# The end of a two-block transformer kernel: the last four experts of the mixture taken apart from the loop, their sums left in PSUM

## The chip, the cores and the metric

The kernel runs on one core of a Trainium2 chip. The metric is device time in microseconds (us) of one execution, the median over several runs. Everything is fp32 in memory. TensorE (PE) multiplies, VectorE (DVE) and ScalarE (ACT) move and combine, GpSimd (POOL) takes roots, SyncE (SP) issues the DMAs of the weights and of the output.

## The reference, cut to what matters

Two transformer blocks follow each other; the second one ends with a mixture of 64 experts, added to the residual, and a last normalization. Only this end is touched.

```
def hier_moe(h, w_group, w_expert, w1, w3, w2):       # 512 tokens, D = 1024, 64 experts, top 2
    ...                                               # gates[token, 2], expert_id[token, 2]
    def expert_block(args):
        xb, e = args
        hid = jax.nn.silu(xb @ w1[e]) * (xb @ w3[e])  # w1, w3: 1024 x 256
        return hid @ w2[e]                            # w2: 256 x 1024
    ys = lax.map(expert_block, (xs, block_e)).reshape(n_slots, dm)
    ys = ys * slot_gate[:, None].astype(ys.dtype)
    out = jnp.zeros((n_tok + 1, dm), ys.dtype).at[slot_tok].add(ys)[:n_tok]
...
    x = x + hier_moe(h, ...)
    return rmsnorm(x, final_norm)
```

## The kernel before, in words

Each expert gets C = 32 places for tokens; one that has more tokens gets an extra block, in a loop behind a branch on `n_over` (the number of extra blocks). Four experts make a bunch (BUNCH = 4) of 128 places, so there are 16 bunches (BUNCHES = 16).

For each expert `b` the kernel does this:
- SP loads W1 and W3 (`gate_up_in`, two DMAs of 1 MB, six slots) and W2 (`down_in`, one DMA of 1 MB, five slots). The order on SP is the gate-and-up weights of expert e+1, then the down weights of expert e. A slot's DMA waits for the PE step that used the slot last.
- PE `gate_up` (L1769): 32 matmuls, four at a time on 32 columns of the array each, into bank 2 or 3. ACT takes the silu (L1104), DVE the product (L2500), PE transposes it (`hidden`, L1783), DVE copies that out (L2520), PE `down` (L1797): 8 matmuls of 32x256 into bank 6 or 7, one quarter of the columns for each 32 partitions. ACT and DVE copy two quarters each into the rows of `Y` (L1110 and L2506).

For each bunch the four experts' rows are brought back to tokens: ACT makes the gated high half of `Y` (`Yhi`, L1127), DVE the rest (`Ylo`, L2525), and PE multiplies both with the 128x512 one-hot places `S4` (`by_token`, L1822 and L1823, two fp32r matmuls for each of 8 tiles, tile = 128 tokens x 512 columns). DVE adds each tile from bank 0 or 1 to the residual `xres` in SBUF (L2539). The two banks alternate, so the matmul of tile i waits for the addition of tile i-2. This work of bunch g-1 is spread over the experts of bunch g.

The last bunch has nothing to be spread over. Its sum is taken once at the end in full fp32: PE multiplies `gated_places` with `Y` (L1961, 8 matmuls), DVE adds each tile (L2539), ACT sums the squares of each 128 tokens (L806), DVE and POOL make the reciprocal root (L2621, L2668), DVE scales (L2616, `finish`), and SP stores (L775 and L779). The branch on `n_over` stands on each engine between the last expert and these matmuls (L1927 on PE). In the profiled execution the loop behind it isn't run: the trace has no row of its lines.

Fillers (`idle_turns`, L1816) are matmuls whose result nobody reads.

The order on each engine is the order of the code; there is no scheduler. Engines wait for each other by semaphores.

## Time and profile before

| | us |
|---|---|
| median of 3 runs | 1454.14 (1452.13 to 1454.15) |
| span of the profiled execution | 1449.5 |
| PE busy | 1386.8 (96%) |
| DVE busy, ACT busy | 526.3, 522.3 |
| DMA | 293.22 MB, mean 202 GB/s |

No time of its own is listed for the profiled execution; two of the three runs took 1454.14 and 1454.15, which is 4.6 us more than its span, for what lies around the span. Matmuls are pipelined and their ends are modelled, so a busy share of PE says little by itself. Where an fp32 matmul stands in a row, the count is of two records for each instruction: the 32 matmuls of `gate_up` are x64.

### The profile page before, as it was taken

Reading aid. Unit: us, or ns where it says so; the run is one execution under the profiler, and the core shown is the slowest. Engines: PE = TensorE matmul, PEld = TensorE weight load, DVE = VectorE, ACT = ScalarE, POOL = GpSimd, SP = SyncE. Lnnn points to the kernel's source line nnn. Section 1 sums busy time; section 2 is a strip of 40 time slices with the busy share of each in tenths; the row PEclk is TensorE's granted clock in tenths of the full one; section 3 lists DMA queues with packets and bytes.
Section 4 is the critical chain, followed back from the end, with each engine's and each line's share of the span. In section 5 each row is a group of like instructions: output and inputs, shape, how many; then the busy total and the mean of one; then the engine's idle time right before and its main releaser. Section 6 shows DMA issues by size and latency. Waiting matters only on the chain. (4 is left out here: it accounts for less than half of the span.)

```text
span 1449.5 us, 26659 instructions
## 1 busy us (share of the span) xinstructions
PE 1386.8 (96%) x11116; PEld 1038.9 (72%) x11116; DVE 526.3 (36%) x1256; ACT 522.3 (36%) x1096; POOL 474.6 (33%) x457
## 2 busy tenths in 40 slices
PE   6999999999999999999989999999999999889986
PEld 5788886668788888888868786866666665555553
DVE  3102107752221200221244604264554554454435
ACT  4325438863422322322345533342223222222222
POOL 5334545553544444444355854410000000000000
PEclk9999999999999999999999999999999999999999
DMA  5133215304133124231232311669999999999994
GB/s 188 59 118 116 96 59 173 112 16 160 58 117 105 41 94 153 73 116 61 89 116 73 106 69 59 241 253 382 410 419 419 419 419 420 419 420 420 420 420 183
DMA packets 89561, 293.22 MB, mean 202 GB/s; under 512 B 9308, under 2 KB 38144, under 8 KB 64864
## 3 DMA queue, kind: packets, MB, share of 16 engines
q1 hardware_dynamic: 89040, 290.35, 51.9%
q8 instruction: 90, 1.47, 0.4%
q0 software_dynamic: 288, 1.05, 0.2%
q14 instruction: 31, 0.25, 0.0%
q10 hardware_dynamic: 112, 0.09, 0.0%
HBM read 289.27 MB, written 2.13 MB: 201 GB/s over the span
## 5 line engine op out<-in xcount | busy, mean ns | idle before, releaser
L496 POOL TENSOR_TENSOR wring_halves<-wring,wring_halves 128x512 fp32r<-128x512 f32 x274 | 356.6, 1306 | 379.9 <-ACT wring_halves L491 378.2
L491 ACT CAST wring_halves<-wring 128x512 fp32r<-128x512 f32 x274 | 168.3, 621 | 433.2 <-PE ps L1223 412.2
L1221 PE MATMUL ps<-wring_halves,big_halves 128*128 128x512 f32 x612 | 241.6, 395 | 3.7 <-POOL wring_halves L496 2.6
L1221 PE MATMUL ps<-hT_halves,wring_halves 128*128 128x512 f32 x480 | 187.4, 390 | 2.4 <-DVE big_halves L1981 2.4
L1222 PE MATMUL ps<-big_halves,wring_halves 128*128 128x512 f32 x480 | 186.8, 389 | 0.0
L1223 PE MATMUL ps<-hT_halves,wring_halves 128*128 128x512 f32 x480 | 186.7, 389 | 0.0
L2668 POOL TENSOR_TENSOR rstd<-rstd,half 128x1 f32<-128x1 f32 (+1 forms) x21 | 13.6, 647 | 507.7 <-DVE rstd L2621 478.5
L1222 PE MATMUL ps<-wring_halves,hT_halves 128*128 128x512 f32 x436 | 170.7, 391 | 0.0
L1223 PE MATMUL ps<-wring_halves,hT_halves 128*128 128x512 f32 x436 | 170.6, 391 | 0.0
L1221 PEld LDWEIGHTS ps<-wring_halves,big_halves 128*128 128x128 f32 x612 | 115.4, 189 | 31.9 <-POOL wring_halves L496 5.7
L1742 PE MATMUL ps<-xn,fixed 128*128 128x512 f32 x256 | 119.2, 608 | 1.1 <-DVE fixed L2416 1.1
L1221 PEld LDWEIGHTS ps<-hT_halves,wring_halves 128*128 128x128 f32 x480 | 90.1, 188 | 22.5 <-POOL wring_halves L496 2.9
L1223 PEld LDWEIGHTS ps<-hT_halves,wring_halves 128*128 128x128 f32 x480 | 90.1, 188 | 18.9
L1222 PEld LDWEIGHTS ps<-big_halves,wring_halves 128*128 128x128 f32 x480 | 90.1, 188 | 18.8 <-issue 0.2
L2506 DVE COPY arena<-ps 32x256 f32<-32x256 f32 x128 | 54.3, 425 | 120.6 <-PE ps L1797 116.0
L1223 PEld LDWEIGHTS ps<-wring_halves,hT_halves 128*128 128x128 f32 x436 | 82.3, 189 | 17.6
L1222 PEld LDWEIGHTS ps<-wring_halves,hT_halves 128*128 128x128 f32 x436 | 82.5, 189 | 16.5
L2539 DVE TENSOR_TENSOR xres<-xres,ps 128x512 f32<-128x512 f32 x128 | 82.5, 683 | 22.1 <-PE ps L1823 18.0
L2160 DVE TENSOR_TENSOR arena<-arena,ps 128x512 f32<-128x512 f32 x22 | 15.0, 684 | 195.4 <-ACT arena L971 195.4
L1742 PEld LDWEIGHTS ps<-xn,fixed 128*128 128x128 f32 x256 | 46.3, 191 | 54.6 <-issue 52.3
L1769 PE MATMUL ps<-big,arena 128*32 128x128 f32 x2048 | 65.9, 279 | 8.8 <-DMA big<-in_moe_w_dram 8.2
L1110 ACT COPY arena<-ps 32x256 f32<-32x256 f32 x128 | 46.3, 361 | 64.2 <-PE ps L1797 63.5
(348 smaller groups left out, 1986.3 us busy)
## 6 DMA issues: line engine op xcount, KB each, us to landing
big<-in_moe_w_dram SPq DMA_DIRECT2D x90, 1024.0 KB, 24.7
wring<-in_moe_w_dram SPq DMA_DIRECT2D x70, 1024.0 KB, 25.2
wring<-in_ffn_w_in_dram SPq DMA_DIRECT2D x22, 1024.0 KB, 7.3
hT<-in_moe_w_dram SPq DMA_DIRECT2D x20, 1024.0 KB, 24.3
wring<-in_fox_w_in_dram SPq DMA_DIRECT2D x7, 2048.0 KB, 8.7
wring<-in_gla_w_in_dram SPq DMA_DIRECT2D x6, 2048.0 KB, 7.9
mkv<-in_moe_w_dram SPq DMA_DIRECT2D x12, 1024.0 KB, 26.1
wring<-in_ffn_w_out_dram SPq DMA_DIRECT2D x4, 2048.0 KB, 7.8
```

The source lines that it names most:

```text
L491: act.copy(hi, src).then_inc(s_hi, 1)
L496: pool.tensor_tensor(lo, src, hi, ALU.subtract).then_inc(s_lo, 1)
L1110: last = act.copy(rows[:, n * YG:(n + 1) * YG], bank(6 + j % 2)[n * C:(n + 1) * C, 0:YG])
L1221: pe.matmul(out, lhs[1], rhs[0], start=start, stop=False)
L1222: pe.matmul(out, lhs[0], rhs[1], start=False, stop=False)
L1223: return pe.matmul(out, lhs[0], rhs[0], start=False, stop=stop)
L1742: last = pe.matmul(bank(n), one_hots(g)[1][:, t, :], xn[:, t, n * 512:(n + 1) * 512], start=(t == 0), stop=(t == T - 1))
L1769: last = pe.matmul(o[i * C:(i + 1) * C, 0:2 * HG], xeT[:, k, r * C:(r + 1) * C], w[:, :, i // 2, :, i % 2], start=(k == 0), stop=(k == KD ...
L2160: dve.tensor_tensor(prod[f % 2], sg[f % 2], bank((2 * f + 1) % 8), ALU.mult).then_inc(s_hid, 1)
L2506: last = dve.tensor_copy(rows[:, n * YG:(n + 1) * YG], bank(6 + j % 2)[n * C:(n + 1) * C, 0:YG])
L2539: dve.tensor_tensor(d, d, bank(n), ALU.add).then_inc(done, 1)
L2668: rooted.inc(pool.tensor_tensor(v, v, half[0:v.shape[0], 0:v.shape[1]], ALU.pow))
```

## The change

It leaves experts 0 to 59 in the loop (`LB` = 60) and writes out the last four by themselves.

1. SP: the down weights of expert 62 are issued before the gate-and-up weights of expert 63, and these come in four DMAs of 512 KB instead of two of 1 MB: first the first half of the contraction of W1 and W3, then the second half, with a semaphore of its own (`s_l13`). PE multiplies the first half when that is in (`last_in(3, range(KD // 2))`).
2. The by-token sums of bunch 14 are added to the residual by DVE and written into PSUM banks 0 to 6 (seven of the eight tiles; the eighth, in bank 7, goes to `xres` as before). The eight idle matmuls in bank 0 stand ahead of them. The last bunch's experts use bank 2 and 3 for gate and up of the first two, and a part of bank 7 (`work`) for all the rest.
3. `three_experts`: experts 60 to 62 are gated into `Yhi` and `Ylo` (96 rows) while the last weights arrive, and their matmuls add onto the banks (`start=False`).
4. `last_expert`: the down result of expert 63 is copied once as it stands, 64 partitions by ACT and 64 by DVE (`y_quarters`), and multiplied with a copy of its places in all four groups of 32 partitions (`last_places`), in 14 fp32 matmuls of 32 rows x 256 columns, in four rounds of 4, 3, 4 and 3.
5. The eighth tile is still one full fp32 matmul of all four experts, and one addition.
6. ACT squares and DVE `finish` read three and a half row tiles straight from PSUM.
7. The branch stands after the copy-out of expert 63's transposed hidden rows and ahead of its `down`. The register for it is loaded at expert 58 instead of 62.

Outside the last four experts there is only renaming of semaphores.

The last DMA issues on SP, before (`wring` in the first rows holds experts 62 and 63's gate and up; the two L740 at the end are the down weights of 62 and 63):

```order
L740 DMA big<-in_moe_w_2_dram 128x2048 [waits moe_y]
L734 DMA wring<-in_moe_w_2_dram 128x2048 [waits moe_gate_up]
L734 DMA wring<-in_moe_w_2_dram 128x2048
L740 DMA big<-in_moe_w_2_dram 128x2048 [waits moe_y]
L734 DMA wring<-in_moe_w_2_dram 128x2048 [waits moe_gate_up]
L734 DMA wring<-in_moe_w_2_dram 128x2048
L740 DMA wring<-in_moe_w_2_dram 128x2048 [waits moe_y] x2
```

and now, where L808 are the four halves:

```order
L779 DMA big<-in_moe_w_2_dram 128x2048 [waits moe_y]
L773 DMA wring<-in_moe_w_2_dram 128x2048 [waits moe_gate_up]
L773 DMA wring<-in_moe_w_2_dram 128x2048
L779 DMA big<-in_moe_w_2_dram 128x2048 [waits moe_y]
L779 DMA wring<-in_moe_w_2_dram 128x2048 [waits moe_y]
L808 DMA wring<-in_moe_w_2_dram 128x1024 [waits moe_gate_up]
L808 DMA wring<-in_moe_w_2_dram 128x1024 x3
L779 DMA wring<-in_moe_w_2_dram 128x2048 [waits moe_y]
```

Down weights of expert 62 moved ahead of expert 63's gate and up; the last megabyte is the same.

PE from expert 63's gate and up to the branch, before (L1769 gate and up, L1783 hidden transposed, L1797 down of 62 and of 63):

```order
L1816 MATMUL ps<-fixed_halves 128x512 x6
L1769 MATMUL ps<-wring,arena 32x128 [waits moe_xT_out,moe_hidden,expert_gate_up_in_3]
L1769 MATMUL ps<-wring,arena 32x128 x15
L1769 MATMUL ps<-wring,arena 32x128 [waits moe_xT_out]
L1769 MATMUL ps<-wring,arena 32x128 x15
L1783 MATMUL ps<-ident,arena 64x64 [waits moe_hiddenT_out,moe_hidden]
L1783 MATMUL ps<-ident,arena 64x64
L1797 MATMUL ps<-wring,arena 32x256 [waits moe_y_out_act,moe_y_out_dve,expert_down_in_2,moe_hiddenT_out]
L1797 MATMUL ps<-wring,arena 32x256 x7
L1797 MATMUL ps<-wring,arena 32x256 [waits moe_y_out_act,moe_y_out_dve,expert_down_in_3,moe_hiddenT_out]
L1797 MATMUL ps<-wring,arena 32x256 x7
L1927 COMPARE_AND_BRANCH [waits moe_y_added]
```

and now (L1993 gate and up, L2026 three_experts, L1861 hidden):

```order
L1993 MATMUL ps<-wring,arena 32x128 [waits expert_gate_up_in_3,last_bunch_y_out_dve,last_bunch_y_out_act]
L1993 MATMUL ps<-wring,arena 32x128 x15
L1993 MATMUL ps<-wring,arena 32x128 [waits last_gate_up_second_half_in]
L1993 MATMUL ps<-wring,arena 32x128 x15
L2026 MATMUL ps<-arena_halves,fixed_halves 128x512 [waits moe_y_added,last_bunch_y_out_dve,last_bunch_y_out_act]
L2026 MATMUL ps<-arena_halves,fixed_halves 128x512
L1861 MATMUL ps<-ident,arena 64x64 [waits last_bunch_hidden]
L1861 MATMUL ps<-ident,arena 64x64
L2026 MATMUL ps<-arena_halves,fixed_halves 128x512 x2
L2079 COMPARE_AND_BRANCH [waits last_bunch_hiddenT_out]
```

The down step of 62 is gone from here (it runs earlier), two tiles of `three_experts` stand around the transpose, and the branch has come ahead of expert 63's down step. After it PE now has this, where before there were the eight L1961 in a row (L1875 down of 63, L2037 the 32-row products):

```order
L1875 MATMUL ps<-wring,arena 32x256 [waits expert_down_in_3,last_bunch_hiddenT_out]
L1875 MATMUL ps<-wring,arena 32x256 x7
L2026 MATMUL ps<-arena_halves,fixed_halves 128x512 x4
L2037 MATMUL ps<-hT 128x256 [waits last_bunch_y_out_dve,last_bunch_y_out_act,last_places_gated]
L2037 MATMUL ps<-hT 128x256 x3
L2026 MATMUL ps<-arena_halves,fixed_halves 128x512 x4
L2037 MATMUL ps<-hT 128x256 x3
L2037 MATMUL ps<-hT 128x256 [waits last_bunch_row_tiles_done]
L2037 MATMUL ps<-hT 128x256 x3
L2026 MATMUL ps<-arena_halves,fixed_halves 128x512 x2
L2037 MATMUL ps<-hT 128x256 [waits last_bunch_row_tiles_done]
L2037 MATMUL ps<-hT 128x256 x2
```

Only one full matmul (L2121) follows.

DVE at the end, before (L2539 additions, L2621 the mean square, L2616 finish):

```order
L2539 TENSOR_TENSOR xres<-xres,ps 128x512 [waits moe_y_by_token,moe_y_added] x2
L2621 TENSOR_SCALAR rstd<-ss 128x1 [waits squares_summed]
L2539 TENSOR_TENSOR xres<-xres,ps 128x512 [waits moe_y_by_token,moe_y_added]
L2616 SCALAR_TENSOR_TENSOR xres<-xres,rstd,gainrow 128x1024 [waits root_taken]
L2539 TENSOR_TENSOR xres<-xres,ps 128x512 [waits moe_y_by_token,moe_y_added]
L2621 TENSOR_SCALAR rstd<-ss 128x1 [waits squares_summed]
L2539 TENSOR_TENSOR xres<-xres,ps 128x512 [waits moe_y_by_token,moe_y_added]
L2616 SCALAR_TENSOR_TENSOR xres<-xres,rstd,gainrow 128x1024 [waits root_taken]
```

and now the whole of it (L2808 and L2811 copy expert 63's rows, L2840 the one addition, L2834 finish):

```order
L2808 COPY hT<-ps 64x256 [waits last_bunch_y]
L2811 COPY arena<-hT 32x256 [waits last_bunch_y_out_dve]
L2811 COPY arena<-hT 32x256
L2824 TENSOR_SCALAR rstd<-ss 128x1 [waits squares_summed,later_gainrow_in]
L2840 TENSOR_TENSOR xres<-xres,ps 128x512 [waits moe_y_by_token]
L2824 TENSOR_SCALAR rstd<-ss 128x1 [waits squares_summed]
L2834 SCALAR_TENSOR_TENSOR xres<-ps,rstd,gainrow 128x1024 [waits root_taken]
L2824 TENSOR_SCALAR rstd<-ss 128x1 [waits squares_summed]
L2834 SCALAR_TENSOR_TENSOR xres<-ps,rstd,gainrow 128x1024 [waits root_taken]
L2820 TENSOR_SCALAR both_eps<-ss 128x1 [waits squares_summed]
L2822 TENSOR_SCALAR rstd<-ss,both_eps 128x1 [waits squares_summed,dve_self]
L2834 SCALAR_TENSOR_TENSOR xres<-ps,rstd,gainrow 128x1024 [waits root_taken]
```

Seven of the eight additions at the end are gone; finish reads `ps`.

The diff, cut to what is spoken of:

```diff
@@ SyncE
-            for e in range(D_SLOTS, EXPERTS):
-                if e + 1 < EXPERTS:
-                    gate_up_in(e + 1, (e + 1) % E_SLOTS, e + 2 - E_SLOTS)
+            for e in range(D_SLOTS, EXPERTS - 2):
+                gate_up_in(e + 1, (e + 1) % E_SLOTS, e + 2 - E_SLOTS)
                 down_in(e, e % D_SLOTS, e + 1 - D_SLOTS)
+            e = EXPERTS - 1
+            down_in(e - 1, (e - 1) % D_SLOTS, e - D_SLOTS)
+            sp.wait_ge(s_gu, e + 1 - E_SLOTS)
+            last_in = w13_slot(e % E_SLOTS)
+            for i in range(2):
+                ks = slice(i * KD // 2, (i + 1) * KD // 2)
+                for g, src in enumerate((W1, W3)):
+                    sp.dma_start(last_in[:, g, ks, :].rearrange("p k n -> p (k n)"), src[e][:, i * KD // 2 * FF:(i + 1) * KD // 2 * FF]).then_inc(s_l13 if i else s_e13[e % E_SLOTS], 16)
+            down_in(e, e % D_SLOTS, e + 1 - D_SLOTS)
@@ ScalarE
+            last_silu(0)
+            y_of(LB - 1)
+            bunch_high(BUNCHES - 2)
...
+            act.activation(gated_places, S4[(BUNCHES - 1) % 3].bitcast(F32), ACT.Copy, scale=gatecol[:, BUNCHES - 1:BUNCHES]).then_inc(s_S4g, 1)
+            last_silu(1)
+            last_y_of(0)
+            act.wait_ge(s_S4g, 1)
+            for n in range(4):
+                last = act.copy(last_places[n * C:(n + 1) * C, :], gated_places[LAST * C:(LAST + 1) * C, :])
...
+            last_silu(2)
+            last_y_of(1)
+            last_y_of(2)
...
+            act.activation(Yhi[rows, :], Y[rows, :], ACT.Copy, scale=gatecol[rows, BUNCHES - 1:BUNCHES]).then_inc(s_lyA, 1)
+            last_silu(LAST)
             with act.If(n_over > 0):
...
-            for t in range(T):
-                act.wait_ge(s_add, 8 * (BUNCHES - 1) + 2 * t + 2)
-                squares(6, t, xres[:, t, :])
+            act.wait_ge(s_ly, BUNCH)
+            act.copy(y_quarters[0:2 * C, :], work_y[0:2 * C, :]).then_inc(s_lyA, 1)
+            for t in range(T - 1):
+                act.wait_ge(s_lrt, 3 + t // 2)
+                squares(6, t, bank(2 * t, 2))
...
+            act.activation(scr[0][:, 0:512], bank(6), ACT.Square, accum_out=ss[:, T - 1:T]).then_inc(s_ss, 1)
+            act.wait_ge(s_add, 8 * (BUNCHES - 1) + 1)
+            act.activation(scr[0][:, 512:D], xres[:, T - 1, 512:D], ACT.Square, accum_out=ss[:, T:T + 1]).then_inc(s_ss, 1)
@@ TensorE
+            def three_experts(i):
+
+                t, n = divmod(i, 2)
+                rows = slice(0, LAST * C)
+                for half in (Ylo, Yhi):
+                    pe.matmul(bank(i), S4[(BUNCHES - 1) % 3][rows, t * P:(t + 1) * P], half[rows, n * 512:(n + 1) * 512],
+                              start=False, stop=False, skip_group_check=True)
+
+            ROUNDS = [[(0, 0), (0, 2), (1, 1), (1, 3)], [(2, 0), (2, 2), (3, 1)],
+                      [(0, 1), (0, 3), (1, 0), (1, 2)], [(2, 1), (2, 3), (3, 0)]]
+
+            def last_expert(i):
+
+                wait(pe, s_lrt, i - 1)
+                for t, n in ROUNDS[i]:
+                    q = slice(n * C, (n + 1) * C)
+                    last = pe.matmul(bank(2 * t + n // 2)[:, n % 2 * YG:(n % 2 + 1) * YG], last_places[q, t * P:(t + 1) * P],
+                                     y_quarters[q, :], start=False, stop=True, skip_group_check=True)
+                last.then_inc(s_lrt, 1)
...
+            last_in(0, range(KD))
+            expert_out(LB - 1)
+            last_hidden(0)
...
+            for _ in range(8):
+                pe.matmul(bank(0), S4[(BUNCHES - 1) % 3][:, 0:P], S4[(BUNCHES - 1) % 3], start=True, stop=True)
+            pe.wait_ge(s_yl, BUNCHES - 1)
+            for n in range(4):
+                bunch_before(n)
+            last_in(1, range(KD))
...
+            last_down(0)
+            bunch_before(4)
+            last_hidden(1)
+            bunch_before(5)
+            bunch_before(6)
+            y_read(0)
+            last_in(2, range(KD))
+            pe.wait_ge(s_lhTe, 2)
+            bunch_before(7)
+            last_hidden(2)
+            pe.wait_ge(s_lhTe, 3)
+            last_down(1)
+            y_read(1)
+            last_down(2)
+            y_read(2)
+            last_in(3, range(KD // 2))
+            last_in(3, range(KD // 2, KD))
+            y_read(LAST)
             pe.wait_ge(s_add, 8 * (BUNCHES - 1))
+            three_experts(0)
+            last_hidden(3)
+            three_experts(1)
+            pe.wait_ge(s_lhTe, BUNCH)
             with pe.If(n_over > 0):
...
-            for i in range(8):
-                t, n = divmod(i, 2)
-                wait(pe, s_add, 8 * (BUNCHES - 1) + i - 1)
-                pe.matmul(bank(n), gated_places[:, t * P:(t + 1) * P], Y[:, n * 512:(n + 1) * 512], start=True, stop=True).then_inc(s_cm, 1)
+            last_down(3)
+            three_experts(2)
+            three_experts(3)
...
+            last_expert(0)
+            three_experts(4)
+            three_experts(5)
+            last_expert(1)
+            last_expert(2)
+            three_experts(6)
+            last_expert(3)
+            pe.wait_ge(s_lyD, BUNCH + 2)
+            pe.matmul(work, gated_places[:, (T - 1) * P:T * P], Y[:, 512:D], start=True, stop=True).then_inc(s_cm, 1)
@@ VectorE
+            def rows_added(n):
+
+                i = BEFORE[n]
+                dve.wait_ge(s_cm, 8 * (BUNCHES - 2) + n + 1)
+                dve.tensor_tensor(row_sums(i), xres[:, i // 2, i % 2 * 512:(i % 2 + 1) * 512], before_bank(i), ALU.add).then_inc(s_add, 1)
...
+            rows_added(4)
+            last_hT_out(1)
+            rows_added(5)
+            rows_added(6)
+            rows_added(7)
+            last_hid(2)
+            last_hT_out(2)
+            last_y_of(1)
+            last_y_of(2)
...
+            dve.scalar_tensor_tensor(out=Ylo[rows, :], in0=Y[rows, :], scalar=gatecol[rows, BUNCHES - 1:BUNCHES], in1=Yhi[rows, :],
+                                     op0=ALU.mult, op1=ALU.subtract).then_inc(s_lyD, 1)
+            last_hid(LAST)
+            last_hT_out(LAST)
```

## Rows read from the trace of the kernel before

**Rows 1.** Page, chain that ended last, its end: start us, length us, what.

```profile
1397.99 26.93 DMA wring<-in_moe_w_dram
...
1424.97 2.10 PE ps L1769 x60
...
1428.96 0.98 issue
1429.93 1.10 PE ps L1797 x16
...
1432.18 4.52 PE ps L1961 x6
```

**Rows 2.** Timeline, gate-and-up matmuls of experts 59, 61 and 62: start, length, engine, what, idle before.

```profile
1395.17 3.57 PE L1769 MATMUL ps<-hT,arena 128*32 128x128 f32 x64 [3.04 <-DMA hT<-in_moe_w_dram]
...
1410.09 2.03 PE L1769 MATMUL ps<-big,arena 128*32 128x128 f32 x64 [0.52 <-DMA big<-in_moe_w_dram]
...
1417.55 2.02 PE L1769 MATMUL ps<-wring,arena 128*32 128x128 f32 x64 [1.91 <-DMA wring<-in_moe_w_dram]
```

**Rows 3.** Timeline, SP's last two weight issues.

```profile
1400.17 4.30 SPq L740 DMA_DIRECT2D wring<-in_moe_w_dram  x2
```

**Rows 4.** Timeline, expert 63's silu to its down step, and the copies after it.

```profile
1427.09 0.22 ACT L1104 ACTIVATE arena<-ps 128x64 f32<-128x64 f32 x1 [3.49 <-PE ps L1769]
1427.35 0.22 DVE L2500 TENSOR_TENSOR arena<-arena,ps 128x64 f32<-128x64 f32 x1 [3.26 <-ACT arena L1104]
1427.62 0.34 PE L1783 MATMUL ps<-ident,arena 128*64 128x64 f32 x4 [0.60 <-DVE arena L2500]
1428.01 0.23 DVE L2520 COPY arena<-ps 128x64 f32<-128x64 f32 x1 [0.44 <-PE ps L1783]
1431.06 0.87 DVE L2506 COPY arena<-ps 32x256 f32<-32x256 f32 x2 [1.17 <-PE ps L1797]
1432.15 0.30 PEld L1961 LDWEIGHTS ps<-arena,fixed 128*128 128x128 f32 x2 [1.63 <-issue]
```

**Rows 5.** Windows: stretch, us, PE, PEld, DVE, ACT, POOL busy, PE clock, DMA share, GB/s.

```profile
1434.00:1435.00 1.00, 1.00 (x2) 0.29 (x1) 0.57 (x1) 0.00 (x0) 0.00 (x0) 0.50 0.00 0
...
1437.00:1438.00 1.00, 1.00 (x3) 0.30 (x2) 0.96 (x3) 0.43 (x2) 0.29 (x1) 1.00 0.00 0
```

**Rows 6.** Timeline, the last additions, squares, roots, scalings and stores.

```profile
1440.24 1.98 PE L1961 MATMUL ps<-arena,fixed 128*128 128x512 f32 x4 [0.71 <-DVE xres L2539]
...
1442.78 0.68 DVE L2539 TENSOR_TENSOR xres<-xres,ps 128x512 f32<-128x512 f32 x1
1442.94 0.55 POOL L2668 TENSOR_TENSOR rstd<-rstd,half 128x1 f32<-128x1 f32 x1 [2.06 <-DVE rstd L2621]
1443.48 1.06 ACT L806 ACTIVATE arena<-xres 128x1024 f32<-128x1024 f32 x1 [1.46 <-DVE xres L2539]
1443.52 1.28 DVE L2616 SCALAR_TENSOR_TENSOR xres<-xres,rstd,gainrow 128x1024 f32<-128x1024 f32 x1
1444.45 0.19 ACT L806 ACTIVATION_READ_ACCUMULATOR arena<-xres 128x1 f32 x1
1444.72 0.15 DVE L2621 TENSOR_SCALAR rstd<-ss 128x1 f32<-128x1 f32 x1
...
1445.53 1.42 DVE L2616 SCALAR_TENSOR_TENSOR xres<-xres,rstd,gainrow 128x512 f32<-128x512 f32 x2 [0.66 <-POOL rstd L2668]
```

**Rows 7.** Timeline, bunch 14's gating (L1127, L2525).

```profile
1408.81 1.15 ACT L1127 ACTIVATE arena_halves<-arena 128x1024 fp32r<-128x1024 f32 x1 [0.31 <-DVE arena L2506]
...
1410.09 1.29 DVE L2525 SCALAR_TENSOR_TENSOR arena_halves<-arena,arena_halves 128x1024 fp32r<-128x1024 f32 x1 [0.25 <-ACT arena_halves L1127]
```

**Rows 8.** Timeline, filler matmuls of the fp32r kind.

```profile
1405.05 1.65 PE L1816 MATMUL ps<-fixed_halves 128*128 128x512 f32 x6
```

**Rows 9.** Timeline, fp32 products on 64 rows (the first block's attention) and on 32.

```profile
250.65 0.74 PE L1385 MATMUL ps<-arena 64*128 64x144 f32 x8
...
223.67 0.69 PE L1411 MATMUL ps<-mkv 32*128 32x256 f32 x2 [0.55 <-ACT wring L920]
```

More of the change, by code:

```diff
@@ L626, in gate_sums @@
             v, g2, more = (0, 1, 2) if isinstance(g, int) and g == 0 else (2, 0, 1)
-            return tuple(bank(5)[:, i:i + 1] for i in (v, g2, more))
+            return tuple(bank(5 if isinstance(g, int) else 7)[:, i:i + 1] for i in (v, g2, more))
         turned_at = [arena[:, a:a + KD * P] for a in (1440, 3712, 4736, 3712)]
@@ L1086, in tokens_out @@
                 act.wait_ge(s_G, g * 2 + n + 1)
-                act.copy(G[:, n * 512:(n + 1) * 512], bank(n)).then_inc(s_Ge, 1)
+                act.copy(G[:, n * 512:(n + 1) * 512], bank(n if isinstance(g, int) else 7)).then_inc(s_Ge, 1)
             def xT_out(g, i, b):
@@ L1109, in y_out @@
                 for n in range(2):
-                    last = act.copy(rows[:, n * YG:(n + 1) * YG], bank(6 + j % 2)[n * C:(n + 1) * C, 0:YG])
+                    last = act.copy(rows[:, n * YG:(n + 1) * YG], y_at(b)[n * C:(n + 1) * C, :])
                 last.then_inc(s_myA, 1)
@@ L1734, in gate_column @@
                 for t in range(T):
-                    last = pe.matmul(bank(5)[:, 0:3], one_hots(g)[1][:, t, :], gate_inputs(g)[:, column(0, t), :], start=(t == 0), stop=(t == T - 1))
+                    last = pe.matmul(bank(5 if isinstance(g, int) else 7)[:, 0:3], one_hots(g)[1][:, t, :], gate_inputs(g)[:, column(0, t), :], start=(t == 0), stop=(t == T - 1))
                 last.then_inc(s_gcP, 1)
@@ L1741, in tokens @@
                 for t in tiles:
-                    last = pe.matmul(bank(n), one_hots(g)[1][:, t, :], xn[:, t, n * 512:(n + 1) * 512], start=(t == 0), stop=(t == T - 1))
+                    last = pe.matmul(bank(n if isinstance(g, int) else 7), one_hots(g)[1][:, t, :], xn[:, t, n * 512:(n + 1) * 512], start=(t == 0), stop=(t == T - 1))
                 if t == T - 1:
@@ L1830, in bunch_by_token @@
                 wait(pe, s_add, 8 * g + i - 1)
-                by_token(i, S4[g % 3], Yhi, Ylo, s_cm)
+                by_token(bank(i % 2), i, S4[g % 3], Yhi, Ylo, s_cm)
             pe.wait_ge(s_hnrow, T)
@@ L1924, in _, with last_in @@
                 hidden_of(b)
-            expert_out(EXPERTS - 1)
+            def last_in(r, ks):
+                e = LB + r
+                if r < LAST or ks[0] == 0:
+                    pe.wait_ge(s_e13[e % E_SLOTS], 32 * (e // E_SLOTS + 1))
+                else:
+                    pe.wait_ge(s_l13, 32)
+                w13 = w13_slot(e % E_SLOTS)
+                for k in ks:
+                    if r == 0 and k % 4 == 0:
+                        pe.wait_ge(s_xT, 2 * (BUNCHES - 1) + k // 4 + 1)
+                    w = w13[:, :, k, :].rearrange("p g (h n q) -> p g h n q", h=2, q=KF)
+                    for i in range(4):
+                        last = pe.matmul(last_gate_up_at(r)[i * C:(i + 1) * C, :], xeT[:, k, r * C:(r + 1) * C], w[:, :, i // 2, :, i % 2],
+                                         start=(k == 0), stop=(k == KD - 1), skip_group_check=True)
+                if k == KD - 1:
+                    last.then_inc(s_lgu, 1)
@@ new lines, in _ @@
+                    pe.wait_ge(s_mhid, i + (LB + 1))
+                    hidden(work_h, 0).then_inc(s_mhT, 1)
+                    pe.wait_ge(s_mhTe, i + (LB + 1))
+                    pe.wait_ge(s_e2[X_D], i * 16 + 16 * (LB // D_SLOTS + 1))
+                    down(work_y, 0, X_D).then_inc(s_my, 1)
+                    pe.wait_ge(s_yl, i + BUNCHES)
+                    for n in range(2 * T - 1):
+                        v = S4[BUNCHES % 3][0:C, n // 2 * P:(n // 2 + 1) * P]
+                        for half in (Yolo, Yohi):
+                            pe.matmul(bank(n), v, half[:, n % 2 * 512:(n % 2 + 1) * 512], start=False, stop=False, skip_group_check=True)
@@ L2505, in y_out @@
                 for n in range(2, 4):
[L2506 removed]
+                    last = dve.tensor_copy(rows[:, n * YG:(n + 1) * YG], y_at(b)[n * C:(n + 1) * C, :])
                 last.then_inc(s_myD, 1)
@@ L2609, in _ @@
[L2609 to L2617 removed]
+                    hid(i + LB, 0)
@@ new lines, in mean_square, with finish @@
+                root_of_row[t] = roots.n
+            def finish(t):
+                dve.wait_ge(s_pw, root_of_row[t])
+                if t < T - 1:
+                    parts = [(slice(0, D), bank(2 * t, 2))]
+                else:
+                    parts = [(slice(0, 512), bank(6)), (slice(512, D), xres[:, t, 512:D])]
+                for c, src in parts:
+                    dve.scalar_tensor_tensor(out=xres[:, t, c], in0=src, scalar=rstd[:, t:t + 1], in1=gainrow[:, c],
+                                             op0=ALU.mult, op1=ALU.mult).then_inc(s_fin, 1)
@@ L2630, in _ @@
+            mean_square(0)
+            dve.wait_ge(s_cm, 8 * (BUNCHES - 1) + 1)
+            d = xres[:, T - 1, 512:D]
+            dve.tensor_tensor(d, d, work, ALU.add).then_inc(s_add, 1)
+            mean_square(1)
+            finish(0)
+            mean_square(2)
+            finish(1)
             mean_square(T - 1)
+            finish(2)
             finish(T - 1)
```

299 lines of the change are left out of this document (169 added, 130 removed).

## The prediction, as it was recorded before the changed kernel was run

> **What bounds the kernel now.** I read the page first. PE is busy 96% of the time, but the change touches only the last 50 of 1449.5 us, so I went to the end of the chain of waits. There the reader should see two things. Up to 1424.97 the chain is DMA: expert 63's gate and up weights land, 26.93 us after their issue [rows 1]. The matmuls of 61, 62 and 63 start at 1410.09, 1417.55 and 1424.97 [rows 1, 2], 7.45 us for 3 MB, or 2.48 us for each MB of a queue that is never empty. PE waits for it. Behind expert 62's down step PE stands still for 0.98 us and starts expert 63's at 1429.93 [rows 1]; everything else that it needs was ready at 1428.24 (1428.01 + 0.23 [rows 4]), so this is the last megabyte landing, at about 1429.9. Second, from there to the end of the span are 19.6 us with no weights to wait for: the tail. Its order is down (to 1431.0), copies (to 1431.93), eight fp32 matmuls that alternate over two banks with eight additions, then squares, root, scaling and store. The windows show PE's clock at 0.50 around 1434.5, the lower of its two levels (1.2 GHz), and 1.00 at 1437 [rows 5]: PE had stood still around the last down step (0.98 us before it, 1.1 us behind it). The last scaling ends at 1446.95 (1445.53 + 1.42 [rows 6]); the span ends 2.55 us later with the last store.
>
> **The sum's base.** The span is 1449.5; 1454.14 is 4.64 more. I keep 4.64 and the 2.55 of the store, since neither is touched. So only the end of the last scaling has to be forecast.
>
> **SP and the stream.** The issue order changes, the volume doesn't, and the last megabyte is the same one, so I let it land at 1429.9 again. Expert 63's second half takes the place in which the down weights of 62 were, one MB earlier: 1429.9 - 2.5 = 1427.4. Two more DMAs are issued. An issue takes 2.15 us (4.30 for two [rows 3]), so the last is issued at about 1408.7 in place of 1404.5; it has 21 us before it can land, so this is hidden (if each issue cost double, it still is). Halved pieces could run slower; nothing in the rows shows 512 KB weight loads. Bounds 0 and +0.5 us (a tenth of 2 MB), I take 0. The load of the branch register moves from expert 62 to 58; it stands in PE's, ACT's and DVE's queue ahead of expert 58's work, and PE's wait of 3.04 us for expert 59 [rows 2] covers it.
>
> **Before the last weights.** PE's new list between 1410 and 1427 is full, so I went through it. The seeds of PSUM take as many additions as before (0.68 each, to PSUM instead of SBUF: not shown, bounds 0 and +0.2 each, I take 0). Gate and up of 62 can run at 1417.6, when they land, to 1419.6. Then: eighth tile of bunch 14, two fp32r matmuls (1.65 for six [rows 8], so 0.25 each), and its addition, which DVE does ahead of 62's product (0.5 + 0.7); product, transpose and copy-out (0.25 + 0.35 + 0.3); 1421.8. Down of 61, 1.07, copies 0.87 and their waits: 1423.95. Down of 62 and copies, which share one bank and so follow each other: 1426.0. Yhi 1.15 and Ylo 1.29 [rows 7], with 0.1 between: 1428.7. Expert 63's second half is multiplied from 1427.45 to 1428.5. The first three_experts tile waits for Ylo: 1428.7 to 1429.25; product meanwhile (silu and product took 0.5 [rows 4]); transpose to 1429.6, copy-out 1429.95. So this list ends where the last megabyte lands: no gain and no loss, with no slack either. Each 1 us by which it is late is 1 us at the end; bounds -0 (DMA holds it) and +2 (the two down steps and their copies once more).
>
> **The branch.** It was hidden: PE's last down matmul had been started by 1431.0, DVE's copies ended at 1431.93, and PE loaded weights at 1432.15 [rows 4]. So a branch costs at most 1.1 us. Now it stands open between the copy-out (1430.0) and the down step. Bounds 0 and 1.1; 0.5, the middle, as the row fits both: down from 1430.6 to 1431.65, which is 0.65 later than before. ACT's and DVE's branches come earlier than their next work by over 1 us and are hidden. The Trainium skill (Advanced Engine Details and Errata, Control Flow Timing) gives about 108 ns for a compare-and-branch; with that the time would be 0.4 lower. Its page Runtime: NRT & Kernel Launch (Instruction fetch mechanics) says that a taken branch out of the fetched window stalls for a fetch by DMA, with no price, which speaks for the upper end. No row here separates them.
>
> **The tail.** Behind down of 63 the path is: two tiles of three_experts, four matmuls, 1.0 us. They cover the copies of the quarters (64 partitions x 256, about 0.45, one each on ACT and DVE where it was two each in 0.87 [rows 4]). Then a round of four 32-row products, 1.0 of fp32r, two rounds. Price of a round: an fp32 matmul of 512 columns takes about 0.9 (two in 1.98 with a wait [rows 6]), so 256 columns 0.43. If the four run beside each other, a round is 0.43; if in line, 1.7. The attention's products on 64 rows, four instructions of 144 columns, took 0.74 from first start to last end [rows 9]; in line they would take 4 x 0.25 plus about 0.17 of draining, 1.15. So two row groups do run side by side. I take 0.55, nearest to that row. The Trainium skill (TensorE: Matmul & The Clock Gate, Part 3) measured 3.07 times for four 32-row tiles; that gives 4 x 0.43 / 3.07 = 0.56. No row of before shows four.
> Sum: 1431.65 + 1.0 + 0.55 + 1.0 + 0.55 + 0.55 = 1435.3: four banks and two more are complete, ACT can square. Two squares at 1.06 + 0.19 [rows 6]: 1437.95. The eighth tile's matmul ends by 1437.4 and its addition by 1438.1, beside that. Then DVE is in line with itself: mean square 0.15, finish 1.28, 0.15, 1.28, 0.3, 1.28, and 1.42 for the last two halves [rows 6], 5.9 us. Squares (to 1440.9) and roots (0.55 [rows 6]) are beside it. End: 1438.15 + 5.9 = 1444.05, against 1446.95: 2.9 less.
> In parts: +0.65 up to the end of down, and 12.4 instead of 15.95 us from there. What goes is the slow clock in the first matmuls, and seven additions of 0.68 that DVE made between its scalings. What is late next is DVE with its four scalings.
> Reading PSUM in finish and squares, 1024 elements: additions with one operand in PSUM took 0.68 for 512, scalings from SBUF 1.28 for 1024 [rows 6], so at most 0.1 each.
>
> **Predicted: 1454.14 - 2.9 = 1451.2 us**, which is 0.20% faster.
>
> **Rivals.**
> 1. *The small terms are small.* Branch 0.1 and a round 0.45: 0.4 + 3 x 0.1 off, 1450.4. For: nothing on PE is known to be slower. Against: modes change seven times in the tail.
> 2. *The list before is late, or the clock falls.* The copies through the one bank come late by 1 to 2 us, or PE's waits around the branch bring the clock to 1.2 GHz again, which doubles PE's parts of the path. From 1431.65 that is 3.65 us if it lasted all through, 1 to 2 if in part. For: the windows show it once in the tail [rows 5]. Against: PE now has work before and behind the branch. 1452.8.
> 3. *The 32-row products run one after another: slower.* Place: the rounds. Eleven of them stand before the squares. At 0.43 each it is 4.7 instead of 1.65, and the last round moves the eighth tile too: +3.8, 1455.0. At 0.69 each, what one alone took [rows 9], 7.6 instead of 1.65: 1457.1. From 0.41 each the change loses. For: no row shows more than two row groups at once. Against: that row, and that each round writes different banks.
> 4. *The change doesn't do what it says:* halving expert 63's load buys nothing, since the last megabyte holds the end. My sum holds this already at no gain.
>
> **How the numbers follow.** A measurement of this kernel can tell 0.2%, 2.9 us. Forecast 48% (own range 1450.5 to 1452.2; its middle is on the line, and I put 28 on faster as the slow start of the tail is surely gone), rival 1 20% (faster), rival 2 20% (same 19, slower 1), rival 3 12% (same 4, slower 8). Faster 0.48, same 0.43, slower 0.09. The range 1449.6 to 1454.9 goes from rival 1 with a branch at nothing to the lower end of rival 3.
>
> **What would show it.** Right: expert 63's gate and up in two pieces, the second at about 1427.4; down at 1430.6 with an issue gap before it; a round of 32-row products 0.5 to 0.6 long; no clock of 0.50 behind 1430; squares from 1435.3; four scalings almost without gaps. Wrong: a first three_experts tile behind 1429.5, rounds over 1 us, a DMA stream that ends at another time than 1429.9, or a gap of over 1 us at the branch.

## The result, and the profile after

The changed kernel is slower by 0.4%: 1457.95 us (median of 8 runs, 1453.37 to 1462.45) against 1452.58 for the kernel before in 8 runs beside it. The ratio is 1.004, 95% interval 1.0027 to 1.0054. The forecast was 1451.2, in a range up to 1454.9. (One run of before took 2740.22 us; it is left out of the ratio, and without it the median of before is 1452.13.)

The end of the chain of waits of the changed kernel, start, length and what:

```profile
1425.69 1.12 PE ps L1993 x32
1426.81 0.09 issue
1426.90 0.71 PE ps L2026 x2
1427.61 0.27 PE ps L1861 x4
1427.88 0.67 PE ps L2026 x2
1428.54 3.53 issue
1432.07 1.93 PE ps L1875 x16
1434.01 2.01 PE ps L2026 x4
1436.01 1.17 PE ps L2037 x8
1437.18 2.01 PE ps L2026 x4
1439.18 2.01 PE ps L2037 x14
...
1443.51 2.02 PE ps L2121 x2
```

Read it against the end of the chain of before [rows 1]. Up to 1428.54 all is as intended: the second half of expert 63's gate and up (L1993), two tiles of three_experts (L2026) around the transpose (L1861). Then PE waits 3.53 us for nothing that the profile shows, at the branch. The last megabyte had landed at 1428.1. Every PE row behind it is nearly twice as long as it should be: expert 63's down step takes 1.93 instead of 1.10 [rows 1]. The windows say why (columns as in [rows 5]); first the changed kernel:

```profile
1428.00:1432.00 4.00, 0.54 (x2) 0.10 (x1) 0.15 (x1) 0.00 (x0) 0.00 (x0) 0.78 0.02 4
1432.00:1436.00 4.00, 3.93 (x24) 1.90 (x24) 1.00 (x3) 0.36 (x1) 0.00 (x0) 0.50 0.02 4
1436.00:1440.00 4.00, 4.00 (x21) 2.44 (x23) 0.00 (x0) 0.00 (x0) 0.00 (x0) 0.50 0.00 0
1440.00:1444.00 4.00, 4.00 (x19) 1.91 (x16) 0.15 (x1) 2.55 (x5) 0.56 (x1) 0.50 0.00 0
```

The granted clock goes to 0.50, the lower of its two levels (1.2 GHz), during the gap and doesn't come back while PE is busy for 13 us. It is not this profile alone: the mean granted clock of the eight runs is 0.983 to 0.990, and 0.989 to 0.996 in the twelve runs of a_shortbody below, which executes the same instructions. In the kernel before it was at 0.50 for a part of the eight L1961 only, and at 1.00 again by 1437 [rows 5].

So relative to the stream of weights (expert 58's matmuls start at 1384.83 here, at 1386.19 before) the down step starts 3.5 us later than before, and from it to the end of the last scaling are 19.5 us (1432.07 to 1451.57) where before there were 17.0 (1429.93 to 1446.95) and the sum had 13.45.

### The profile page after: what moved, and what is told of

It reads as the page before. It is cut to its first block and busy times, and to the rows that moved or that the text cites. A ratio compares the mean times of both kernels' runs of the same rounds, so it can differ in the third digit from the quotient of the medians.

```text
span 1454.7 us, 26668 instructions
## 1 busy us (share of the span) xinstructions
PE 1387.6 (95%) x11134; PEld 1039.6 (71%) x11134; DVE 523.4 (36%) x1253; ACT 525.2 (36%) x1102; POOL 475.4 (33%) x457
## 3 DMA queue, kind: packets, MB, share of 16 engines
q8 instruction: 90, 1.47, 0.4%
## 5 line engine op out<-in xcount | busy, mean ns | idle before, releaser
L1300 PE MATMUL ps<-wring_halves,big_halves 128*128 128x512 f32 x612 | 241.3, 394 | 3.8 <-POOL wring_halves L504 2.6
L2666 DVE COPY arena<-ps 32x256 f32<-32x256 f32 x120 | 50.9, 424 | 115.2 <-PE ps L1875 110.9
L2699 DVE TENSOR_TENSOR xres<-xres,ps 128x512 f32<-128x512 f32 x112 | 72.0, 684 | 18.7 <-PE ps L1896 18.2
L1301 PE MATMUL ps<-wring_halves,big_halves 128*128 128x512 f32 x176 | 68.5, 389 | 0.0
L1302 PE MATMUL ps<-wring_halves,big_halves 128*128 128x512 f32 x176 | 68.5, 389 | 0.0
```

The costliest lines, as they stand in the source:

```text
L1300: pe.matmul(out, lhs[1], rhs[0], start=start, stop=False)
L1301: pe.matmul(out, lhs[0], rhs[1], start=False, stop=False)
L1302: return pe.matmul(out, lhs[0], rhs[0], start=False, stop=stop)
L2666: last = dve.tensor_copy(rows[:, n * YG:(n + 1) * YG], y_at(b)[n * C:(n + 1) * C, :])
L2699: dve.tensor_tensor(d, d, bank(n), ALU.add).then_inc(done, 1)
```

## What the branch waits for

The DMA query of a stretch counts instruction packets: queue q8, one packet at a time. The page of the profile has 90 of them with 1.47 MB, so 16 KB each; PE's 22,268 recorded matmuls and weight loads in 90 packets, with waits besides, make about 250 instructions for a packet. So the queue is read here as PE's, and PE's code arrives in blocks. In the last 56 us before the branch one packet comes each 8 to 12 us and takes 1.1 us. The row for the changed kernel from 1428.6 to 1432, columns packets, MB, share of 16 engines:

```profile
q8 instruction: 1, 0.02, 2.4%
```

There is no such packet from 1420 to 1428.6. It starts at 1429.25, behind the branch, and PE starts again 2.8 us later.

The branch has a row of its own, which the chain doesn't show (shortest, median and longest in ns, first and last start). In the changed kernel and in the kernel before:

```profile
L2079 PEldq COMPARE_BRANCH  x1: 3716/3716/3716, 1428.2 to 1428.2; - x1
L1927 PEldq COMPARE_BRANCH  x1: 1474/1474/1474, 1430.0 to 1430.0; - x1
```

The packet of the changed kernel takes 1.29 us, to 1430.54 (2.4% of 16 engines over 3.4 us), and the row of the branch ends at 1431.90, 1.37 behind it. In the kernel before the packet runs from 1428.81 to 1430.12, and the branch's row ends at 1431.48, 1.36 behind it. The table below has this for every run: where a packet was on its way, or had just landed, the branch's row ends 1.36 to 1.38 us behind the packet's end (1.71 in b_longbody, with two packets); where the last packet had landed over 1.7 us before the branch, the row lasts 0.39 to 0.49. So the branch waits for a packet, and it did so before too, for 1.47 us beside the down step and the copies. The Trainium skill (Runtime: NRT & Kernel Launch, Instruction fetch mechanics) says that instructions come in blocks of 256 which are fetched ahead in order only, and that a taken branch out of the window has to wait for the fetch of its target; the trace agrees with that, with a packet that starts 1.06 us behind the start of the branch's row.

By a count from the code, the loop that the branch jumps over has some 300 instructions of PE (its fp32 matmuls count four each). So the jump spans more than one block, and whether its target is in the next block or in the one after depends on where in its block the branch happens to stand. That is theory A. Theory B: a branch on PE costs 3.5 us wherever it lands, and was hidden before. For the clock: A1, it fell because PE stood still; A2, the new 96-row and 32-row products can't hold it.

## The experiments

Each is compared with the kernel before on the same chip in the same session. All ratios are to before; the changed kernel's is 1.0040.

| kernel | us, median | ratio, 95% interval | gap at the branch, us | branch's row, us | its end behind the last packet's end, us |
|---|---|---|---|---|---|
| before | 1451.45 to 1452.58, by session | 1 | hidden | 1.47 | 1.36 |
| changed | 1457.95 | 1.0040 (1.0027 to 1.0054) | 3.53 | 3.72 | 1.37 |
| b_longbody | 1453.09 | 1.0011 (1.0000 to 1.0022) | 3.33 | 4.92 | 1.71 |
| a_shortbody | 1449.01 | 0.9981 (0.9970 to 0.9993) | 0.20 | 0.39 | 9.6 |
| a_nobranch | 1448.02 | 0.9976 (0.9963 to 0.9990) | none | none | |
| a_tiles | 1449.68 | 0.9990 (0.9981 to 0.9998) | filled with work | 1.31 | 1.36 |
| a_fill | 1451.18 | 1.0001 (0.9987 to 1.0016) | filled with 3.2 | 1.18 | 1.36 |
| a_fullrows | 1454.48 | 1.0019 (1.0007 to 1.0032) | 3.75 | 3.94 | 1.38 |
| b_nobranch | 1448.98 | 0.9993 (0.9978 to 1.0007) | none | none | |
| a_pad | 1453.95 | 1.0024 (1.0010 to 1.0039) | 0.31 | 0.49 | 2.8 |
| a_pad12 | 1450.09 | 1.0014 (0.9992 to 1.0036) | 1.20 | 1.38 | 1.36 |
| a_pad12_tiles | 1447.43 | 0.9976 (0.9966 to 0.9987) | filled with work | 2.09 | 1.38 |
| a_short_whole | 1450.82 | 1.0004 (0.9991 to 1.0017) | under 0.3 | 0.39 | 8.7 |
| a_pad12_fill | 1448.47 | 0.9979 (0.9968 to 0.9990) | under 0.4 | 0.48 | 2.3 |

The ratio isn't the quotient of the two medians, and differs from it by 0.2% in a_pad12.

### The loop made longer in the kernel before: b_longbody

```diff
                 with pe.Fori(0, n_over) as i:
+                    idle_turns(110)
                     gate_column(i + BUNCHES)
```

> The kernel before with 110 filler matmuls added inside PE's extra-block loop, which is not run with these inputs: no instruction more is executed, only the branch jumps over 220 more. Theory A (the place of the target: PE's instructions arrive in blocks of 256, one 16 KB packet each, and a jump past the next block has to fetch its target): the branch now lands two blocks on, PE stands still for about 3.5 us at it instead of being hidden, its clock is 0.50 for much of the tail, and the time rises by 2 to 5 us, to 1454.5 to 1457.5. Theory B (the branch costs the same wherever it lands; it was hidden before and is open now): no change, within 0.5 us.

Not one instruction more is executed. The chain of waits behind the last copy:

```profile
1430.25 0.44 DVE arena L2507
1430.69 3.33 issue
1434.02 6.27 PE ps L1962 x10
```

Before, PE loaded weights 0.22 us behind that copy [rows 4]; now 3.33. From 1429.5 to 1430 there are two instruction packets (starts 1429.59 and 1429.92), the regular one and, 0.3 us later, one more:

```profile
q8 instruction: 2, 0.03, 46.9%
```

Theory B can't make this. The time rose by about 1.6 us (0.11%), less than the 2 to 5 expected, and its interval just touches no change. In this profile hardly anything of the gap is hidden: from the last megabyte's landing (1428.52) to L1962 are 5.5 us, where before there were 2.3 (1429.84 to 1432.18). Nor did the clock stay low for much of the tail, as expected: it was at 0.50 from 1433.6 to 1437.0, for as long as before. Why the runs lost only half of what the profile shows is open.

### The loop made shorter in the changed kernel: a_shortbody

```diff
-                    gate_up(work_gu, X_GU, 0, lambda k: None)
+                    pe.matmul(work_gu, xeT[:, 0, :], xeT[:, 0, 0:2 * HG], start=True, stop=True).then_inc(s_gu, 1)
```

> The changed kernel with the 32 gate-and-up matmuls of PE's extra-block loop replaced by one: the loop would compute wrongly, but it isn't run with these inputs, and nothing that is executed changes. Theory A (target within the next block of 256): the gap of 3.53 us before expert 63's down step falls under 1 us, the clock doesn't fall, the time is 1449 to 1452. Theory B (a branch costs 3.5 us anywhere): gap and time as in the changed kernel, 1458. A third theory, that 32-row and 96-row products alone let the clock fall: gap small but clock 0.50 in the tail, 1453 to 1455.

```profile
1429.37 0.76 PE ps L2026 x2
1430.13 0.27 PE ps L1861 x4
1430.39 0.67 PE ps L2026 x2
1431.06 0.20 issue
1431.26 1.07 PE ps L1875 x16
```

The gap is gone, and there is no instruction packet between 1421 and 1432. Its windows:

```profile
1428.00:1432.00 4.00, 3.80 (x52) 2.31 (x44) 0.62 (x3) 0.22 (x1) 0.00 (x0) 0.81 0.00 0
1432.00:1436.00 4.00, 4.00 (x38) 2.37 (x30) 1.00 (x3) 0.37 (x1) 0.00 (x0) 1.00 0.03 8
```

The same products at a clock of 1.00. The ratio falls from 1.0040 to 0.9981, by some 8.6 us, with nothing changed in what is executed. That is the whole of the loss and, in size, the forecast's gain.

### No branch: a_nobranch and b_nobranch

Edit: `with ...If(n_over > 0):` and its block taken out on all four engines, in the changed kernel and in before; extra blocks are left out.

> The changed kernel without the branch and its loop on all four engines (the extra blocks are left out; there are none with these inputs). A and B both: no gap, down of 63 follows the copy-out or the last landing at once, 1449 to 1451.5, some 7 us under the changed kernel. If the clock is low in the tail all the same, the shape of the products does it, and the time is 1452 to 1455.

> The kernel before without branch and loop on all four engines (extra blocks left out, there are none). If the branch was fully hidden there, no change, within 0.5 us of before. If it cost the 0.2 us seen before the first weight load, that much less. A gain of over 1.5 us would say that the comparison of a_nobranch with before was not fair.

a_nobranch (0.9976) lies with a_shortbody, so a branch whose target is there costs next to nothing. b_nobranch is not told apart from before (0.9993, interval over 1). A small gain of the branch's removal in before can't be excluded: its median is low, and in its profile the clock stayed at 1.00 in the tail. Between the two kernels without a branch the change is worth 0.17% (0.9976 against 0.9993), but their intervals overlap, so this comparison alone doesn't tell it from nothing.

### PE kept busy over the gap: a_tiles and a_fill

```diff
             three_experts(1)
+            for i in range(2, 2 * T - 1):
+                three_experts(i)
             pe.wait_ge(s_lhTe, BUNCH)
```

(and the later calls of three_experts taken out), and in a_fill

```diff
             pe.wait_ge(s_lhTe, BUNCH)
+            for _ in range(14):
+                pe.matmul(work, S4[(BUNCHES - 1) % 3][:, 0:P], S4[(BUNCHES - 1) % 3], start=True, stop=True)
             with pe.If(n_over > 0):
```

> The changed kernel with the five remaining tiles of three_experts put ahead of the branch, so that PE has 10 matmuls (2.4 us) queued while the branch is taken. Both theories: the down step starts as late as before, but 2.4 us of PE's work is done in the gap and the idle time falls from 3.5 to about 1.3 us. If the clock falls because PE is idle, it now stays up, and the time falls by 4 to 7 us to 1451 to 1454; if it falls for the shape of the products, only 2 to 3 us, 1455 to 1456.

> The changed kernel with 14 filler matmuls (3.3 us) put in PE's queue right before the branch, behind the wait for the copy-out. The gap at the branch stays (fetch of the target's block), but PE isn't idle in it. Theory A1 (the clock fell because PE stood still): clock 1.00 through the tail, down of 63 still about 4 us late, time 1451.5 to 1453.5, so the gap alone costs 3 to 4 us and the clock the rest. Theory A2 (the 96-row and 32-row products don't hold the clock whatever came before): clock 0.50 in the tail as well, 1456 to 1458.

The chain of a_fill:

```profile
1428.93 0.65 PE ps L2026 x2
1429.59 3.19 PE ps L2080 x14
1432.78 1.00 PE ps L1875 x16
1433.78 1.12 PE ps L2026 x4
```

Both expectations took it that the stall at the branch stays. It doesn't. The rows of the branch in a_fill and in a_tiles:

```profile
L2081 PEldq COMPARE_BRANCH  x1: 1179/1179/1179, 1429.3 to 1429.3; - x1
L2081 PEldq COMPARE_BRANCH  x1: 1314/1314/1314, 1431.1 to 1431.1; - x1
```

They last 1.18 and 1.31 us, not 3.72. The 14 fillers (28 instructions) and the ten matmuls of the tiles (20) stand ahead of the branch in the code and so also move it further on; in both profiles a packet starts 1.2 to 1.6 us ahead of the branch (1427.76, 1429.89), as in a_pad12 below, and the branch only waits for that one. So these two runs don't cover a stall of 3.5 us.

What a_fill does show is the clock. Its down step is at 1432.78 because the fillers (L2080) run until then: a delay of 3.19 us in which PE is busy, in place of one of 3.53 in which it stands still. The down step then takes 1.00, and the clock stays at 1.00 from 1428 to 1444. From the start of the down step to the end of the last scaling are 13.4 us (1432.78 to 1446.15); the changed kernel has 19.5. A1 holds and A2 as stated falls: the 96-row and 32-row products keep a clock that is up. By the ratios of the table, a delay of 3 us costs 0.20% or 2.9 us (a_fill less a_shortbody), and the rest of the loss, 0.39% or 5.7 us (changed less a_fill), is the clock, by the profiles 6.1. The fall of the clock cost twice what the gap did.

a_tiles puts real work there, and gained more than expected (1449.68, where 1451 was the lower end); its interval lies just under 1. How much of that is the work and how much the shorter stall isn't separated.

### All 128 rows: a_fullrows

```diff
-                rows = slice(0, LAST * C)
+                rows = slice(0, P)
```

(in three_experts; expert 63's places then meet an older expert's rows.)

> The changed kernel with three_experts' matmuls over all 128 rows instead of 96 (the last 32 rows hold an older expert's values, so the sums are wrong; the time of a matmul is the same). Gap at the branch as in the changed kernel. If the clock stays at 0.50 for 13 us in the changed kernel because its products use only part of the rows, it comes back to 1.00 within about 4 us here and the time is 1453.5 to 1455.5; if not, clock and time as in the changed kernel, 1457 to 1458.

```profile
1432.00:1436.00 4.00, 3.51 (x20) 1.85 (x20) 1.00 (x3) 0.37 (x1) 0.00 (x0) 0.50 0.01 4
1436.00:1440.00 4.00, 4.00 (x29) 2.19 (x28) 0.00 (x0) 0.12 (x1) 0.00 (x0) 0.81 0.00 0
1440.00:1444.00 4.00, 2.15 (x10) 0.62 (x9) 1.96 (x4) 4.00 (x10) 1.11 (x2) 1.00 0.00 0
```

With a gap as long (3.75), the clock comes back at about 1437.5, and the ratio is 1.0019 against 1.0040. So the shape doesn't let the clock fall, but it seems to have kept it from coming back: with 96 of 128 rows it stayed at 0.50 to the end. That is one profile of each, two intervals that nearly part (1.0007 to 1.0032, 1.0027 to 1.0054), and mean clocks of the runs of 0.987 to 0.994 here against 0.983 to 0.990.

### The complete kernel, moved within its blocks: a_pad, a_pad12

```diff
             pe.wait_ge(s_cst, 1)
+            for _ in range(25):                 # 12 in a_pad12
+                pe.matmul(bank(6)[:, 0:16], ident[:, :], ident[:, 0:16], start=True, stop=True)
             pe.wait_ge(s_gin, 16 * 9)
```

> The changed kernel, complete, with 25 tiny fp32 matmuls (100 instructions of PE) at the very start, where PE waits 9 us for a DMA, so that the branch stands in the next block of 256 and its target in the one after it. Theory A: gap under 1 us, no fall of the clock in the tail, 1448 to 1450.5, as a_shortbody. Theory B: 1458.

> The changed kernel, complete, with 12 tiny fp32 matmuls at the start instead of 25 (48 instructions of PE; the 25 took 10.85 us from 3.68 to 14.5 and pushed everything 5 us back). 12 should end at about 9 us, within the wait for the DMA. If the branch stands some 220 instructions into its block, 48 bring it into the next one: no gap, 1448 to 1450. If the branch stood earlier in its block the target is still two blocks on: gap 3.5 us and 1457.

a_pad missed its time (1453.95) but not its theory. Its chain at the branch:

```profile
1433.89 0.66 PE ps L2028 x2
1434.55 0.31 issue
1434.86 1.07 PE ps L1877 x16
```

The gap is 0.31. The padding itself cost the time: 25 matmuls took 10.85 us from 3.68 on, where PE waited only to 9.2, and the last megabyte lands at 1433.2, 5 us later than in the changed kernel. Twelve end at 8.98, within the wait. But a_pad12's runs fall into two groups, eight from 1445.0 to 1453.0 and four from 1457.5 to 1459.4, and its profile, one of the first group, has a gap of 1.20:

```profile
1429.16 0.65 PE ps L2028 x2
1429.81 1.20 issue
1431.02 1.07 PE ps L1877 x16
```

The regular packet starts at 1428.52, just before this branch, so the branch stands near the head of its block and jumps into one that is still on its way: the packet ends at 1429.48 and the branch's row at 1430.85. Why four runs lose 9 us more was not seen in a profile. That the clock falls in them is on record: their mean granted clock is 0.986 to 0.987, as in the changed kernel, and 0.990 to 0.997 in the other eight. That the gap is longer in them is an inference.

### The best version: a_pad12_tiles, and fillers: a_pad12_fill

a_pad12 with a_tiles' order; and a_pad12 with six fillers of the same kind behind `y_read(0)`, ahead of expert 62's gate and up.

> a_pad12 with the five remaining tiles of three_experts ahead of the branch. With no stall at the branch these 2.4 us of PE's work are in the way of nothing before it only if expert 63's copy-out is late; they now delay the down step by up to 2 us but save 2.2 us behind it. Expect within 0.7 us of a_pad12, 1448 to 1450.5. It should also be the safer one.

> a_pad12 with six filler matmuls (1.5 us) into the free bank while PE waits for expert 62's gate and up. In four of the profiles above the clock was 0.50 somewhere between 1423 and 1430 and the two halves took 3.4 to 3.6 us in place of 2.2. If PE's idle time before it brings the clock down, it stays at 1.00 here and the time is 0.5 to 1.5 us under a_pad12; if the fall comes from the 32-column products, no change.

a_pad12_tiles has the lowest time of the complete kernels, 1447.43, ratio 0.9976, though it isn't told apart from a_pad12_fill (0.9979). Its twelve runs lie within 5.1 us (a_pad12: 14.4). With 10 more matmuls in the queue the branch is taken behind work:

```profile
1427.28 0.71 PE ps L2028 x2
1428.26 3.00 PE ps L2028 x12
1431.26 1.04 PE ps L1877 x16
```

No issue gap, while the branch's row lasts 2.09 (from 1428.57), and the rounds (L2039) follow as 21 rows in 1.64 us. a_pad12_fill also removes the second group of runs (1447.5 to 1450.5), but not for the reason given: its profile has the clock at 0.50 between 1426 and 1428. Its fillers lie ahead of the branch and move it 12 instructions further into its block, which may be what helped: the packet ends at 1428.65, 1.8 us before the branch, whose row lasts 0.48.

### The halves of expert 63's load: a_short_whole

```diff
-            for i in range(2):
-                ks = slice(i * KD // 2, (i + 1) * KD // 2)
-                for g, src in enumerate((W1, W3)):
-                    sp.dma_start(last_in[:, g, ks, :].rearrange("p k n -> p (k n)"), src[e][:, i * KD // 2 * FF:(i + 1) * KD // 2 * FF]).then_inc(s_l13 if i else s_e13[e % E_SLOTS], 16)
+            for g, src in enumerate((W1, W3)):
+                sp.dma_start(last_in[:, g, :, :].rearrange("p k n -> p (k n)"), src[e]).then_inc(s_l13, 16)
```

> a_shortbody with expert 63's gate-and-up weights in two DMAs of 1 MB, still behind the down weights of 62, and PE waiting for both before it starts. If the last megabyte and the copies before it set the end (the recorded sum), the halves buy at most the 1 us of the first half's matmuls: 0 to +1 us against a_shortbody, 1449 to 1450. A loss of over 1.5 us would say that the halves carry the gain.

1.0004 against 0.9981, intervals touching: about 3 us by the ratios, 1.8 by the medians, and 0.9 by the spans of the two profiles (1446.9 and 1447.8, the other way round, since a_shortbody's had its clock down around 1424 to 1429). In the profile the 32 matmuls run from 1426.48 to 1428.55 in one go behind the landing at 1426.35, 1.0 us later than the halves would end. PE also stands still from before 1424 to 1426.4. The 3 us by the ratios are more than the expected 1, and the two profiles don't show where they come from; this is not settled.

## Why the prediction was wrong

**The step that failed** is the one on the branch: "So a branch costs at most 1.1 us. Now it stands open ... Bounds 0 and 1.1; 0.5, the middle". It was 3.53. The bound was read from the end of the down matmuls, but the branch's row doesn't start there: it starts at 1430.01, beside them, and lasts 1.47 us, so in this same trace of before the branch already took more than 1.1. And the bound came from one branch at one place in the code, and was carried to another place. b_longbody shows a gap of 3.33 for that very branch, with only the distance of its target changed. The prediction named the Trainium skill's rule on fetching, saw that it had no price, and gave it no chance of its own. It should have been a rival, with the price of a fetch (a packet's 1 us and the wait around it) and the question of where the target lies. The packets before the branch, which start at 1421.88 and 1428.81 in before, hold a hint: that branch stood early in its block.

**What followed from it** is rival 2, at a larger size. Its place was right (clock at 1.2 GHz around the branch), its chance of 20% and its price, 1 to 2 us, were not. The clock fell for the whole tail, 5.7 us. Even "all through" was put at 3.65, because the down step, the last tile, the last round and the eighth tile's matmul were left out of it; in the changed kernel they stand on the path as well.

**What held.** The stream: the second half of expert 63 was forecast at 1427.4 and the last megabyte at 1429.9; they landed at 1425.65 and 1428.1, and with the 1.36 us by which this profile's stream is early, that is 0.4 early for both. The list before: in the changed kernel it ended at 1428.15 (1427.92 + 0.23), 0.05 us behind the last landing, as forecast without slack. A round of 32-row products was put at 0.55 us: a_shortbody's chain has 0.64 for the first and 1.07 for two, 0.54 each; in the changed kernel 1.17 and 2.01 for two, at half the clock. So rival 3, that they run in line, is wrong: four row groups work side by side. Tail from the start of the down step to the last scaling: forecast 13.45, a_shortbody 13.43 (1431.26 to 1444.69). And its time, at a ratio of 0.9981, is 2.8 us under before (0.19% of 1452, interval 1.0 to 4.4), where the sum said 2.9 less.

**Where luck helped.** The parts of the tail don't agree as its total does. From the end of the down step to the end of the eighth tile's addition, which DVE makes ahead of its first scaling, a_shortbody has 7.0 us (1432.33 to 1439.37) where the sum had 6.5; from there to the end it has 5.3 where the sum had 5.9. The two cancel. In a_shortbody's profile the down step starts 2.6 us behind the last landing (1428.63 to 1431.26), where the sum had 0.7, because the clock was at 0.50 from 1422.7 to 1429.5 and the list before was late; from the last landing to the last scaling that profile is only about 1 us shorter than before (16.1 against 17.1), not 2.9. The 4.64 for what lies around the span is too much: the changed kernel's profiled run took 1456.58 with a span of 1454.7, 1.9 more. It cancels in the 2.9. The two squares from 1435.3 end at 1437.8, not 1437.95, without effect, as the addition ends later.

**Rival 4**, that halving buys nothing, is not supported by a_short_whole, but not refuted either.

The sum's two missing terms are 2.9 for the delay and 5.7 for the clock. With the gain of 2.8 they give the measured +5.8 (0.40% of 1452), but that is no check: the three are differences of the same four ratios and must add up.

## What to carry to other kernels

In these kernels a taken branch on PE was cheap (0.4 to 0.5 us) only when the block with its target had landed well before. Over a body of some 300 instructions that was a matter of where the branch happened to stand, and edits far ahead of it changed the gap from 3.53 to 0.31 or 1.20 us. Independent matmuls queued right before such a branch keep PE busy and its clock up; that they hide a stall is shown for 1.3 and 2.1 us (a_tiles, a_pad12_tiles), not for 3.7. Such an edit also moves the branch, so read the branch's own row before crediting the work that was moved. A bound for a branch is never to be carried from one place of the code to another. When a kernel is slower than its sum, look first for an "issue" gap and for a granted clock of 0.50 behind it: the clock can cost more than the gap that brought it down.

## What was not expected of the hardware

- PE's clock stayed at 0.50 for 13 us of unbroken matmuls over 96 and 32 rows, and came back at about 1437.5 when the larger ones used 128 rows (one profile of each).
- A branch that meets a packet on its way ends 1.36 to 1.38 us behind the packet's end, in seven profiles, whether the gap at the branch is 1.2 or 3.75 us.
- The same code with the same inputs varies by 9 us from run to run in the changed kernel and in before (35 runs), and by 14 us in a_pad12, but by 3 to 6 us where work or fillers stand ahead of the branch (a_tiles, a_pad12_tiles, a_pad12_fill, a_fill).
- The 32 x 256 fp32 products on four row groups take 0.54 to 0.64 us for a round of four, side by side (a_shortbody).
